# Twelve up columns of the dense expert product move into the gate-table stage; the rest runs sixteen columns ahead of the downs, whose sums stay in six PSUM banks

## The chip, the cores and the metric

One core of one Trainium2 chip runs the whole kernel in one launch. The time is device microseconds of that core. Each core has TensorE (matmuls, PE), VectorE (DVE), ScalarE (ACT), GpSimd (POOL) and SyncE (SP, which only issues transfers), an SBUF of 128 partitions, and PSUM with eight banks of 512 fp32 words per partition, into which TensorE writes.

## The reference, cut to what matters

Two layers over 512 tokens of width 1024. Each is a mixer (local attention and a long convolution, gated and projected) and then the expert block that this change is about:

```python
def block(xb):                                  # xb: tokens x 1024, after RMSNorm
    q = (xb @ w_query).reshape(c, 8, 2, 128)
    s = jnp.einsum('chpd,pkd->chpk', q, sub_keys)
    s_top, i_top = lax.top_k(s, 16)
    ...                                         # 16 of 16384 experts per head: idx, softmax weights g
    u = jnp.take(expert_u, idx, axis=0)
    act = jax.nn.gelu(jnp.einsum('chkd,cd->chk', u, xb), approximate=False)
    vsel = jnp.take(expert_v, idx, axis=0)
    return jnp.einsum('chk,chkd->cd', g * act, vsel)
```

All is fp32. A token picks 128 of 128 x 128 experts.

## The kernel before, in words

**Two ways to the same sum.** For the first 384 tokens (three blocks of 128, DT = 384) the block is computed densely: for each of 128 columns j of 128 experts, "up" is gelu(U_j x) for all 384 tokens, it is multiplied by a table G of the softmax weights (zero for experts not picked), and "down" adds the product with V_j. The last 128 tokens take the sparse way: GpSimd gathers their picked rows of U and V from HBM, four buffers of 512 KB (ROWS) going round, and VectorE takes a dot product per gathered row (`dot`, first half of the stage) or adds a weighted row to X (`add_row`, second half). There are 256 gathers per layer.

**fp32 products.** Each dense product is three fp32r matmuls: high x high, high x low, low x high. The high half is a cast (ScalarE, or VectorE for the weights), the low half a subtraction on VectorE. So an up column is 3 x 8 matmuls with 384 moving columns (L874), a down column 3 x 6 with 512 (L889).

**Stages.** The engines meet at numbered barriers (`arrive`, `all_at`). Behind barrier 4 is the table stage: for every token VectorE makes two one-hot rows (L1553, L1554), TensorE multiplies them into a 128 x 128 slice of G (L856), eight banks going round, ScalarE copies it into GST (L1095), and SP stores half tables of 64 tokens to HBM (L488). The one-hots lie in a ring of four groups of eight tokens (OHR). Two U loads and the first two V loads are issued at its start, since their buffers lie apart from those of the stage. Behind barrier 5 is the expert stage. Columns go in groups of four (JG); four up columns are ahead of the downs, in banks 0 to 3. A down takes one output block at a time, twelve matmuls over the four columns of the group, into banks 4 to 7 in turn, and VectorE adds each finished block to X (L1620), six per group.

**Order.** It is written out by hand for each engine and kept by semaphores. In the expert stage a step is a group: TensorE `step`, L894, alternates `up` (L866) and `down` (L878); ScalarE, L1128, does `split_u`, `split_v`, `gelu`; VectorE, L1622, does `split_u`, `split_v`, `weigh` (multiply with the table, cast to high, subtract to low), rows, `add_output`; SP, L497, issues U, V and the table (`load_g`, 768 KB per group); GpSimd's gathers (L573) wait until their buffer was used.

## Time and profile before

| | |
|---|---|
| runs | 3986.62 us median of 3 (3986.41 to 3987.67) |
| profiled execution | 3987.45 us, span 3985.5 us |
| busy share of the span | PE 89%, PEld 71%, DVE 73%, ACT 30%, POOL 22% |
| granted TensorE clock, mean | 0.956 |
| L874 (ups), three groups of 2048 matmuls | 405.8, 399.4, 396.5 us busy |
| L889 (downs), three groups of 1536 | 414.9, 416.5, 412.2 us busy |
| L1620 (adds of down blocks to X) x384 | 263.0 us busy |
| HBM | 672 MB read, 52 MB written, mean 182 GB/s |

Share of busy time is over both layers and all stages; a stage has its own bound. A clock of 1.0 is the full 2.4 GHz. "PEld" is the load of the stationary operand, beside the matmuls. In the timeline a row's "x8" merges eight instructions, and the brackets give the engine's idle time before it and what ended it.

### The profile page before, as it was taken

The page shows a single profiled execution, that of the slowest core. Times are in us where ns is not written, and L with a number is a line of the kernel's source. Part 1 is how long each engine was busy: PE and PEld are TensorE (multiplying, and loading weights), DVE is VectorE, ACT ScalarE, POOL GpSimd, SP SyncE. Part 2 cuts the span into 40 slices and gives each one's busy share as a digit, 9 for nine tenths or more (in the row PEclk, how much of TensorE's full clock was granted, in tenths as well). Part 3 has the DMA queues.
Part 4 walks back from the last instruction along what each step waited for, and adds up shares of the span by engine and source line. Part 5 has one row for each costly group of instructions (what it writes and reads, how often), then busy time and mean ns, then how long its engine had stood idle before and what let it go on. Part 6 is the DMA issues. An engine that isn't in the chain of part 4 may idle for free.

```text
span 3985.5 us, 50340 instructions
## 1 busy us (share of the span) xinstructions
PE 3539.7 (89%) x16330; PEld 2844.3 (71%) x16330; DVE 2925.5 (73%) x6669; ACT 1204.4 (30%) x1804; POOL 896.5 (22%) x661
## 2 busy tenths in 40 slices
PE   7899986468999999999988999845699999999997
PEld 4436753358999999999844377424589999999996
DVE  2443359997888888888724443799978888888887
ACT  2312213353333333333223032224533333333332
POOL 0000007002333333333300000160023333333332
PEclk9989998799999999999999899978999999999999
DMA  3112310236777777777521133103387777777775
GB/s 120 57 32 64 100 66 1 104 149 260 280 276 276 276 276 276 276 276 276 198 95 57 32 80 101 49 1 127 136 299 277 276 276 276 277 275 277 278 277 179
DMA packets 239738, 725.62 MB, mean 182 GB/s; under 512 B 16216, under 2 KB 116824, under 8 KB 204572
## 3 DMA queue, kind: packets, MB, share of 16 engines
q1 hardware_dynamic: 165884, 455.99, 30.4%
q0 software_dynamic: 73760, 268.47, 20.5%
q8 instruction: 48, 0.79, 0.1%
q14 instruction: 46, 0.38, 0.0%
HBM read 671.97 MB, written 52.43 MB: 182 GB/s over the span
## 4 chain that ended last, share of the span: by engine, by line
PE 77%; DVE 16%; ACT 2%; DMA 2%; issue 1%; POOL 1%; SPq 0%; DVEq 0%; POOLq 0%; ACTq 0%
PE ps L874 26%; PE ps L889 26%; PE ps L768 9%; DVE OHS L1554 5%; PE ps L637 4%; DVE OHS L1553 4%; PE ps L818 3%; PE ps L624 2%; PE ps L731 2%; PE ps L756 2%; PE ps L747 1%; PE ps L694 1%; DMA g_table<-GST 1%; PE ps L667 1%; POOL EQ L557 1%
## 5 line engine op out<-in xcount | busy, mean ns | idle before, releaser
L573 POOL DMA_INDIRECT ROWS<-u_rows_dram,GIS x256 | 352.1, 1375 | 704.0 <-DVE STG L1597 640.8
L573 POOL DMA_INDIRECT ROWS<-v_rows_dram,GIS x256 | 345.8, 1351 | 690.0 <-DVE X L1613 635.5
L1120 ACT CAST VHI<-VRAW 128x512 fp32r<-128x512 f32 x512 | 291.8, 619 | 468.9 <-PE ps L889 468.9
L889 PE MATMUL ps<-VHI,WHI 128*128 128x512 f32 x1536 | 414.9, 392 | 2.8 <-DVE WLO L1591 2.8
L889 PE MATMUL ps<-VLO,WHI 128*128 128x512 f32 x1536 | 416.5, 393 | 0.0
L874 PE MATMUL ps<-XHI,UHI 128*128 128x384 f32 x2048 | 405.8, 340 | 11.4 <-DVE ULO L1569 11.4
L889 PE MATMUL ps<-VHI,WLO 128*128 128x512 f32 x1536 | 412.2, 390 | 0.0
L1126 ACT ACTIVATE AC<-ps 128x384 f32<-128x384 f32 x256 | 126.0, 492 | 931.8 <-PE ps L874 931.7
L1620 DVE TENSOR_TENSOR X<-ps,X 128x512 f32<-128x512 f32 x384 | 263.0, 687 | 186.2 <-PE ps L889 186.2
L874 PE MATMUL ps<-XLO,UHI 128*128 128x384 f32 x2048 | 399.4, 336 | 0.0
L874 PE MATMUL ps<-XHI,ULO 128*128 128x384 f32 x2048 | 396.5, 334 | 0.0
L874 PEld LDWEIGHTS ps<-XHI,UHI 128*128 128x128 f32 x2048 | 370.4, 189 | 31.9 <-DVE ULO L1569 12.4
L874 PEld LDWEIGHTS ps<-XLO,UHI 128*128 128x128 f32 x2048 | 362.1, 189 | 0.0
L874 PEld LDWEIGHTS ps<-XHI,ULO 128*128 128x128 f32 x2048 | 359.1, 188 | 0.0
L856 PE MATMUL ps<-OHS 128*128 128x128 f32 x1536 | 232.1, 298 | 126.3 <-DVE OHS L1554 126.2
L889 PEld LDWEIGHTS ps<-VLO,WHI 128*128 128x128 f32 x1536 | 288.6, 188 | 64.8
L889 PEld LDWEIGHTS ps<-VHI,WLO 128*128 128x128 f32 x1536 | 288.9, 188 | 63.1
L1613 DVE SCALAR_TENSOR_TENSOR X<-ROWS,STG,X 128x1024 f32<-128x1024 f32 x256 | 327.0, 1277 | 3.6 <-DMA ROWS<-v_rows_dram,GIS 3.5
L1577 DVE TENSOR_TENSOR VLO<-VRAW,VHI 128x512 fp32r<-128x512 f32 x512 | 329.5, 685 | 0.0
L1569 DVE TENSOR_TENSOR ULO<-URAW,UHI 128x1024 fp32r<-128x1024 f32 x256 | 312.2, 1221 | 15.4 <-ACT UHI L1108 10.6
L1597 DVE CUSTOM_DVE_ANT_0 ROWS<-ROWS,XG 128x1024 f32<-128x1024 f32 x256 | 311.6, 1217 | 14.9 <-DMA ROWS<-u_rows_dram,GIS 14.9
L889 PEld LDWEIGHTS ps<-VHI,WHI 128*128 128x128 f32 x1536 | 284.4, 188 | 46.7 <-issue 3.4
(237 smaller groups left out, 4896.4 us busy)
## 6 DMA issues: line engine op xcount, KB each, us to landing
URAW<-ut_dram SPq DMA_DIRECT2D x128, 1024.0 KB
VRAW<-v_dram SPq DMA_DIRECT2D x128, 1024.0 KB
g_table<-GST SPq DMA_DIRECT2D x12, 4096.0 KB, 11.2
GT<-g_table SPq DMA_DIRECT2D x64, 768.0 KB, 10.0
WR<-w_in_dram SPq DMA_DIRECT2D x8, 2048.0 KB, 13.1
WR<-w_in_dram SPq DMA_DIRECT2D x32, 512.0 KB, 4.7
WR<-w_q_dram SPq DMA_DIRECT2D x8, 2048.0 KB, 8.0
WR<-w_out_dram SPq DMA_DIRECT2D x4, 2048.0 KB, 8.1
```

The lines of the kernel that those rows point to most:

```text
L573: pool.indirect_dma_start(out=ROWS[:, k % GR, :], out_offset=None, in_=table, in_offset=bass.IndirectOffsetOnAxis(ap=GIS[:, par, k:k + 1], ...
L768: last = nc.tensor.matmul(ps[:, bank, :], lhs[a], rhs[c], start=(i == 0 and k == 0), stop=(i == 2 and k == len(pairs) - 1))
L856: last = nc.tensor.matmul(ps[:, n % 8, k * NK:(k + 1) * NK], OHS[:, q % OHR, 0, 4 * s + k, :], OHS[:, q % OHR, 1, 4 * s + k, :], start=Tru ...
L874: last = nc.tensor.matmul(ps[:, jj, 0:DT], a[:, jj, k, :], c[:, k, :], start=(i == 0 and k == 0), stop=(i == 2 and k == KC - 1))
L889: last = nc.tensor.matmul(ps[:, 4 + (g0 + o) % 4, :], a[:, par, jj, b * P:(b + 1) * P], c[:, dh, jj, :], start=(n == 0), stop=(n == 3 * JG ...
L1120: nc.scalar.copy(VHI[:, dh, jj, :], VRAW[:, dh, jj, :]).then_inc(v_hi, 1)
L1554: last = nc.vector.tensor_scalar(OHS[:, q % OHR, 1, c, :], iota, IDS[:, 1, t:t + 1], IDS[:, 2, t:t + 1], ALU.is_equal, ALU.mult)
L1569: nc.vector.tensor_tensor(ULO[:, jj].rearrange("p k i -> p (k i)"), URAW[:, jj // 2, jj % 2, :], UHI[:, jj].rearrange("p k i -> p (k i)"). ...
L1577: nc.vector.tensor_tensor(VLO[:, dh, jj, :], VRAW[:, dh, jj, :], VHI[:, dh, jj, :].bitcast(F32), ALU.subtract).then_inc(v_split, 1)
L1597: nc.vector.tensor_tensor_reduce(ROWS[:, k % GR, :], ROWS[:, k % GR, :], XG[:], 1.0, 0.0, ALU.mult, ALU.add, accum_out=STG[:, par, k:k + 1 ...
L1613: nc.vector.scalar_tensor_tensor(X[:, NB - 1, :], ROWS[:, k % GR, :], STG[:, par, k:k + 1], X[:, NB - 1, :], ALU.mult, ALU.add).then_inc(r ...
L1620: nc.vector.tensor_tensor(xb, ps[:, 4 + (par * NOUT + o) % 4, :], xb, ALU.add).then_inc(out_free, 1)
```

## The change

Columns are handled in pairs (64 pairs, NP). Six pairs (EARLY), twelve columns, have their ups in the table stage: after each group of eight tokens TensorE does six of the 24 matmuls of an up column, in banks 0 and 1, and the table uses banks 4 to 7 only. The one-hot ring shrinks from four groups to two, the loops of 128 tokens are unrolled, and the copy of indices (IDS) goes. The gelu outputs are kept in a ring of sixteen columns (AC), weighed in place, with the low half in place as well (ACL on AC, ULO on URAW, VLO on VRAW). The ups run eight pairs ahead of the downs. A down takes one column at a time, three matmuls into each of six banks (2 to 7), which hold the sums over all 128 columns; X gets them once at the end. The high half of the weights is now a cast on ScalarE. Casts and differences handle a pair (128x2048, or 128x768 for weights) at once. U has four buffers of 1 MB, loaded from the time that the queries' weights are done with; V has four, at addresses used by the table stage (slots 0 and 1 under GST, 2 and 3 behind it), so its first load is issued behind barrier 5. The four rows of a pair are used in a burst at the end of VectorE's step. The last eight pairs have downs alone.

The diff, cut to its core (SP, then TensorE, ScalarE, VectorE):

```diff
-TOK_IT = 128
 CB = 64
-OH, OHR = 8, 4
+OH, OHR = 8, 2
+GB = 4
 JG = 4
 NG = NK // JG
 DB = 3
 DT = DB * P
 NOUT = 2 * DB
+UPB = 8 - NOUT
+NP = NK // 2
+AHEAD = 8
+NQ = DT // OH
+EARLY = NQ // 8
+US, VS, HS2 = 4, 4, 2
+assert UPB == 2 and EARLY == AHEAD - 2 and CB == 8 * OH and NP == 64 and AHEAD == 2 * US == 2 * VS
...
+    AC, _ = sb("AC", [P, 2 * AHEAD, DT])
+    ACL, _ = sb("ACL", [P, 2 * AHEAD, DT], F32R, offset=def_at)
+    ef_at = at[0]
+    GST, _ = sb("GST", [P, 2, NK, CB])
     OHS, _ = sb("OHS", [P, OHR, 2, OH, NK])
-    IDS, _ = sb("IDS", [P, 3, TOK_IT])
-    GST, _ = sb("GST", [P, 2, NK, CB])
+    IDXT, idxt_at = sb("IDXT", [P, 3, DT])
...
+    URAW, _ = sb("URAW", [P, US, 2, KC, P], offset=wr_at)
+    ULO, _ = sb("ULO", [P, US, 2, KC, P], F32R, offset=wr_at)
+    UHI, _ = sb("UHI", [P, HS2, 2, KC, P], F32R, offset=wr_at + 8 * US * DM)
...
+    v_at = max(at[0], ef_at + 8 * NK * CB - 16 * DM)
+    VRAW, _ = sb("VRAW", [P, VS, 2, 2, 512], offset=v_at)
+    VLO, _ = sb("VLO", [P, VS, 2, 2, 512], F32R, offset=v_at)
...
+                sp.wait_ge(pq_out, HP)
+                for p in range(US):
+                    load_u(p, p)
...
+                for h in range(DT // CB):
+                    sp.wait_ge(g_bank_free, CB // 4 * (h + 1))
+                    sp.dma_start(gd[h].rearrange("i j c -> i (j c)"),
+                                 GST[:, h % 2].rearrange("p j c -> p (j c)")).then_inc(g_stored[h % 2], 16)
+                    sp.wait_ge(u_done, 2 * h + 2)
+                    load_u(h + US, h % US)
...
+                load_v(0, 0, 2)
+                load_v(0, 1, 3)
                 g_all_stored(sp)
                 sp.nop().then_inc(sp_at_f, 1)
                 load_g(0, 0)
+                load_v(1, 0, 0)
+                load_v(1, 1, 1)
                 load_g(1, 1)
+                UN = EARLY + US
+                def step(o, g0, i):
+                    p = o + i
+                    if not isinstance(p, int) or p + UN < NP:
+                        sp.wait_ge(u_done, p * 2 + 2 * EARLY + 2)
+                        load_u(p + UN, (i + UN) % US)
+                    if i % 2 == 1 and (not isinstance(p, int) or p // 2 + 2 < NG):
+                        sp.wait_ge(wf_ready, p + 1)
+                        load_g(g0 + i // 2 + 2, i // 2 % 2)
+                    if not isinstance(p, int) or p + VS < NP:
+                        sp.wait_ge(v_out, p * 2 + 2)
+                        load_v(g0 + i // 2 + 2, i % 2, (i + 2) % VS)
...
+                def up(p, i, jj, n0=0, n1=3 * KC):
+                    j = p * 2 + jj
+                    if n0 == 0:
+                        pe.wait_ge(u_split, p + 1)
+                        if not isinstance(j, int) or j >= UPB:
+                            pe.wait_ge(act_ready, j - (UPB - 1))
+                    for n in range(n0, n1):
+                        a, c, k = PASSES[n]
+                        last = nc.tensor.matmul(ps[:, jj, 0:DT], a[:, i % (US if a is ULO else HS2), jj, k, :], c[:, k, :],
+                                                start=(n == 0), stop=(n == 3 * KC - 1))
+                    if n1 == 3 * KC:
+                        last.then_inc(u_done, 1)
+                def down(p, i, jj):
+                    if jj == 0:
+                        pe.wait_ge(w_ready, p + 1)
+                        pe.wait_ge(v_split, p + 1)
+                    wh, wl = WHI[:, (2 * i + jj) % (2 * HS2)], ACL[:, (2 * i + jj) % (2 * AHEAD)]
+                    vh, vl = VHI[:, i % HS2], VLO[:, (i + 2) % VS]
+                    for o in range(NOUT):
+                        dh, b = divmod(o, DB)
+                        for n, (a, c) in enumerate(((wh, vh), (wh, vl), (wl, vh))):
+                            last = nc.tensor.matmul(ps[:, UPB + o, :], a[:, b * P:(b + 1) * P], c[:, dh, jj, :],
+                                                    start=(isinstance(p, int) and p + jj + n == 0),
+                                                    stop=(isinstance(p, int) and 2 * p + jj == NK - 1 and n == 2))
+                    last.then_inc(v_out, 1)
+                for q in range(NQ):
+                    for s in range(OH // 4):
+                        n = q * (OH // 4) + s
+                        pe.wait_ge(oh_ready, n + 1)
+                        if n >= GB:
+                            pe.wait_ge(g_bank_free, n - (GB - 1))
+                        for k in range(4):
+                            last = nc.tensor.matmul(ps[:, 4 + n % GB, k * NK:(k + 1) * NK], OHS[:, q % OHR, 0, 4 * s + k, :],
+                                                    OHS[:, q % OHR, 1, 4 * s + k, :], start=True, stop=True)
+                        last.then_inc(g_out, 1)
+                    up(q // 8, q // 8, q // 4 % 2, q % 4 * 6, q % 4 * 6 + 6)
...
+                def step(o, i, more=True):
+                    for jj in range(2):
+                        down(o + i, i, jj)
                         if more:
+                            up(o + (i + AHEAD), i, jj)
...
+                for p in range(EARLY, AHEAD):
+                    for jj in range(2):
+                        up(p, p, jj)
+                for i in range(8):
+                    step(0, i)
+                with pe.Fori(1, NP // 8 - 1) as it:
+                    for i in range(8):
+                        step(it * 8, i)
+                for i in range(8):
+                    step(NP - 8, i, more=False)
...
+                    for n in range(q * (OH // 4), (q + 1) * (OH // 4)):
+                        h, c = divmod(4 * n, CB)
+                        act.wait_ge(g_out, n + 1)
+                        if c == 0 and h >= 2:
+                            act.wait_ge(g_stored[h % 2], 16 * (h // 2))
+                        nc.scalar.copy(GST[:, h % 2, :, c:c + 4].rearrange("p j c -> p c j"),
+                                       ps[:, 4 + n % GB, :].rearrange("p (c j) -> p c j", c=4)).then_inc(g_bank_free, 1)
+                    if q % 8 == 2:
+                        split_u(q // 8 + 1, q // 8 + 1)
+                    if q % 4 == 1 and q >= 5:
+                        j = q // 4 - 1
+                        gelu(j // 2, j // 2, j % 2)
+                gelu(EARLY - 1, EARLY - 1, 1)
...
+                def step(o, i):
+                    p = o + i
+                    if not isinstance(p, int) or p + AHEAD + 1 < NP:
+                        split_u(o + (i + AHEAD + 1), i + AHEAD + 1)
+                    if not isinstance(p, int) or p + 1 < NP:
+                        split_v(o + (i + 1), i + 1)
+                        high_w(o + (i + 1), i + 1)
+                    if not isinstance(p, int) or p + AHEAD < NP:
+                        for jj in range(2):
+                            gelu(o + (i + AHEAD), i + AHEAD, jj)
+                split_u(EARLY + 1, EARLY + 1)
+                act.wait_ge(g_stored[0], 16 * ((DT // CB + 1) // 2))
+                split_v(0, 0)
+                for jj in range(2):
+                    gelu(EARLY, EARLY, jj)
+                split_u(AHEAD, AHEAD)
+                gelu(AHEAD - 1, AHEAD - 1, 0)
+                high_w(0, 0)
+                gelu(AHEAD - 1, AHEAD - 1, 1)
...
+                    if q >= OHR:
+                        dve.wait_ge(g_out, OH // 4 * (q - OHR + 1))
+                    for c in range(OH):
+                        t = q * OH + c
+                        nc.vector.tensor_scalar(OHS[:, q % OHR, 0, c, :], iota, IDXT[:, 0, t:t + 1], None, ALU.is_equal)
+                        last = nc.vector.tensor_scalar(OHS[:, q % OHR, 1, c, :], iota, IDXT[:, 1, t:t + 1],
+                                                       IDXT[:, 2, t:t + 1], ALU.is_equal, ALU.mult)
+                        if c % 4 == 3:
+                            last.then_inc(oh_ready, 1)
+                    if q % 8 == 4:
+                        split_u(q // 8 + 1, q // 8 + 1)
...
+                def step(o, g0, i, rows):
+                    p, s, par = o + i, g0 + i // 2, i // 2 % 2
+                    if rows is add_row and i % 2 == 0:
+                        stage_weights(s, par)
+                    if not isinstance(p, int) or p + 1 < NP:
+                        n = i + 1
+                        weigh(o + n, n, (o + n) // 4 * 16 + 16 if isinstance(o, int) else o * 4 + (n // 4 * 16 + 16))
+                    if not isinstance(p, int) or p + AHEAD + 1 < NP:
+                        split_u(o + (i + AHEAD + 1), i + AHEAD + 1)
+                    if not isinstance(p, int) or p + 1 < NP:
+                        split_v(o + (i + 1), i + 1)
+                        low_w(o + (i + 1), i + 1)
+                    for k in range(4):
+                        rows(s, par, 4 * (i % 2) + k)
+                    if rows is dot and i % 2 == 1:
+                        keep_dots(s, par)
+                split_u(EARLY + 1, EARLY + 1)
+                split_v(0, 0)
+                split_u(AHEAD, AHEAD)
+                weigh(0, 0, 16)
+                low_w(0, 0)
...
+                for o in range(NOUT):
+                    dh, b = divmod(o, DB)
+                    xb = X[:, b, 512 * dh:512 * dh + 512]
+                    dve.wait_ge(v_out, NK)
+                    nc.vector.tensor_tensor(xb, ps[:, UPB + o, :], xb, ALU.add)
```

## Rows read from the trace of the kernel before

**Rows 1.** The page's chain that ended last: share of the span by engine and line

```profile
PE ps L874 26%; PE ps L889 26%; PE ps L768 9%; DVE OHS L1554 5%; PE ps L637 4%; DVE OHS L1553 4%; PE ps L818 3%; PE ps L624 2%; PE ps L731 2%; PE ps L756 2%; PE ps L747 1%; PE ps L694 1%; DMA g_table<-GST 1%; PE ps L667 1%; POOL EQ L557 1%
```

**Rows 2.** Windows of 50 us: stretch, busy us (instructions) per engine, clock, DMA share, GB/s

```profile
850.00:900.00 50.00, 33.32 (x217) 28.61 (x216) 49.87 (x220) 28.02 (x27) 0.00 (x0) 0.93 0.39 168
1200.00:1250.00 50.00, 50.00 (x255) 45.50 (x254) 42.85 (x73) 15.23 (x24) 17.32 (x13) 1.00 0.78 283
```

**Rows 3.** Timeline, half a group, expert stage, layer 1: start us, us, engine, line, operation

```profile
1934.25 1.57 PE L874 MATMUL ps<-XHI,UHI 128*128 128x384 f32 x8
...
1935.66 1.55 PE L874 MATMUL ps<-XLO,UHI 128*128 128x384 f32 x8
...
1938.44 1.08 PE L889 MATMUL ps<-VHI,WHI 128*128 128x512 f32 x4
...
1950.86 1.57 PE L874 MATMUL ps<-XHI,UHI 128*128 128x384 f32 x8
```

**Rows 4.** Four lines over the whole span: ns min/median/max, first and last start

```profile
L1569 DVE TENSOR_TENSOR ULO<-URAW,UHI x256: 1215/1220/1227, 912.1 to 3921.4; 128x1024 fp32r<-128x1024 f32 x128
...
L1577 DVE TENSOR_TENSOR VLO<-VRAW,VHI x512: 680/685/691, 934.8 to 3952.0; 128x512 fp32r<-128x512 f32 x171
...
L1613 DVE SCALAR_TENSOR_TENSOR X<-ROWS,STG,X x256: 1271/1277/1286, 1476.6 to 3963.5; 128x1024 f32<-128x1024 f32 x128
...
L1126 ACT ACTIVATE AC<-ps x256: 480/492/496, 923.5 to 3939.9; 128x384 f32<-128x384 f32 x128
```

**Rows 5.** Timeline of the table stage, layer 1

```profile
729.13 0.23 DVE L1541 CAST GI<-GIF 128x128 int32<-128x128 f32 x1
...
732.04 0.29 DVE L1553 TENSOR_SCALAR OHS<-CST,IDS 128x128 f32<-128x128 f32 x1
...
734.00 4.78 PE L856 MATMUL ps<-OHS 128*128 128x128 f32 x24 [3.44 <-DVE OHS L1554]
...
790.66 0.55 DVE L1547 COPY IDS<-IDXT 128x384 f32 x1 [0.61 <-DVE OHS L1554]
...
791.35 0.29 DVE L1553 TENSOR_SCALAR OHS<-CST,IDS 128x128 f32<-128x128 f32 x1
...
908.25 0.37 DVE L1554 TENSOR_SCALAR OHS<-CST,IDS 128x128 f32<-128x128 f32 x1
...
908.68 1.16 PE L856 MATMUL ps<-OHS 128*128 128x128 f32 x8 [0.65 <-DVE OHS L1554]
909.87 1.01 ACT L1095 COPY GST<-ps 128x512 f32<-128x512 f32 x1 [0.78 <-PE ps L856]
```

**Rows 6.** Timeline from the table stage into the expert stage, layer 1

```profile
911.06 0.33 SPq L488 DMA_DIRECT2D g_table<-GST  x1
...
913.42 2.93 PE L874 MATMUL ps<-XHI,UHI 128*128 128x384 f32 x8 [3.58 <-DVE ULO L1569]
...
918.56 1.55 PE L874 MATMUL ps<-XHI,ULO 128*128 128x384 f32 x8
...
922.56 1.07 SPq L475 DMA_DIRECT2D GT<-g_table  x2
...
923.84 7.40 SPq L468 DMA_DIRECT2D URAW<-ut_dram  x2
...
932.54 1.04 ACT L1108 CAST UHI<-URAW 128x1024 fp32r<-128x1024 f32 x1 [7.20 <-DMA URAW<-ut_dram]
```

**Rows 7.** DMA issues of the page: KB each, us from issue to landing

```profile
g_table<-GST SPq DMA_DIRECT2D x12, 4096.0 KB, 11.2
```

**Rows 8.** Timeline of the end of the expert stage, layer 1

```profile
1972.84 3.01 POOL L573 DMA_INDIRECT ROWS<-v_rows_dram,GIS  x1 [1.19 <-DVE X L1613]
...
1976.16 0.94 POOL L573 DMA_INDIRECT ROWS<-v_rows_dram,GIS  x1 [0.30 <-issue]
...
1982.89 1.07 PE L889 MATMUL ps<-VHI,WLO 128*128 128x512 f32 x4
...
1986.13 1.28 DVE L1613 SCALAR_TENSOR_TENSOR X<-ROWS,STG,X 128x1024 f32<-128x1024 f32 x1
```

318 lines of the change are left out of this document (91 added, 227 removed).

## The prediction

> **What bounds the kernel now.** I read the chain of waits first, then windows, then the timeline at three seams. The chain is TensorE's two expert lines for 52%, then the one-hots of VectorE for 9% [rows 1]. So two stretches per layer matter. In the table stage (E, 732.04 to 911 in layer 1) VectorE is busy 49.87 of 50 us and TensorE 33.32, with a granted clock of 0.93 [rows 2]: VectorE sets the pace, TensorE has a third of the time free. In the expert stage (F, 913.42 to 1987.41) TensorE is busy 50.00 of 50 us at clock 1.00, VectorE 42.85, the DMA engines 0.78 of the time [rows 2]. The reader should see that what leaves TensorE in F is worth its full price, and what is added to VectorE in E costs its full price.
>
> **TensorE's price of a column.** Ups start at 1934.25 and the next downs at 1938.44: 24 up matmuls take 4.19 us, 0.174 each. From 1934.25 to 1950.86 lie two ups and three of the six down blocks of a group, that is two columns in 16.61 us, 8.305 each [rows 3]. So the downs of a column take 8.305 - 4.19 = 4.115 us.
>
> **Stage E.** Added on VectorE: six differences of 128x2048 (pairs 1 to 6; pair 0 is before the stage). 128x1024 takes 1.22 and 128x512 0.685 [rows 4], so 0.535 for each 512 elements and 1.22 + 2 x 0.535 = 2.29 us for 2048; six are 13.7. Removed: the copies of the indices. Each of the two inside the loop costs a wait of 0.61, the copy of 0.55 and the restart until 791.35, where one-hots follow every 0.23 us: 1.4 us in all, 2.8 for two [rows 5]. The first copy goes too, but pair 0's difference comes before the stage on VectorE: GI is written at 729.36, plus 2.29 and a handshake of 0.3 is 731.95, and the first one-hot stood at 732.04 [rows 5]: nothing gained or lost. The last one-hot ends at 908.62 now [rows 5], so at 908.6 - 2.8 + 13.7 = 919.5.
>
> Does TensorE keep up? It gets 12 columns, 288 up matmuls, six after every eight tokens. Warm: 16 one-hot records in 2 x 1.16 us at most [rows 5] and 6 x 0.174 = 1.04, together 3.4; VectorE needs 3.62 for the same eight tokens (48 such groups in 176.6 - 2.8 us). So the ring of two instead of four is enough, by a narrow margin, and VectorE's splits give TensorE rest. ScalarE adds six wide casts (at most 2 x 1.04 each) and 12 gelus of 0.49 beside 96 copies of 1.01 [rows 4 to 6], some 116 us of 188: hidden, with four banks for a copy every 1.8 us. The stores and U loads in SP's order have 30 us per half table.
>
> The last one-hot matmuls then end near 920.7, the six ups at 921.7, ScalarE's copy at 921.8 and the last gelu at 922.4. TensorE can start F at once, because pair 6 is already split; today it waits for a cast and a difference, from 911.06 to 913.42 [rows 6]. F's first matmul: 922.6, that is 9.2 later.
>
> **Start of F.** Ahead of the first down stand pairs 6 and 7 (four columns). V can't be loaded early any more, since its slots lie where the table stage works. V of pair 0 is issued at about 922.6, behind the last store on SP's queue, issued at 922.0 and landing after 11.2 [rows 6, 7]: 933.2. Then 1 MB: the U load issued at 923.84 behind 1.5 MB issued at 922.56 lets ScalarE go on at 932.54, 2.5 MB in 10.0 us [rows 6]; I take 3.3 us: 936.5. ScalarE waits for it in its own order (split_v ahead of gelu of pair 6), and column 14 needs a bank that this gelu empties. So TensorE does pair 6 until 931.0, then stands still until 936.5 + 1.9 (cast) + 0.5 (gelu) = 938.9, and comes back at the low clock: today sixteen ups after the pause take from 913.42 to 918.56, 0.32 each, 2.35 more than warm [rows 6]. Pair 7: 8.4 + 2.3, so downs begin at 949.6. The weights of pair 0 are ready by then: table load issued at 933.4, landed near 943, weigh 0.95, cast 0.9, difference 0.95, 947. Bounds: if loads of one queue share rather than queue, TensorE goes on until 939.4, waits for weights until about 944 and is cold again: 946.4, 3 better; if the table load lands 10 us later than 943, the weights are ready at 957, 8 worse.
>
> **The run of F.** Per pair TensorE needs 16.61. VectorE: weigh and low_w of 128x768, 0.685 + 0.27 = 0.95 each; two splits of 2.29; four rows of 1.28 [rows 4]: 11.6 against 43/50 of 16.6 = 14.2 today, as the adds out of the banks and the cast of the weights go. ScalarE: two casts of 2, high_w 0.9, two gelus of 0.5: 6. The waits: ScalarE's split of U is released when up of the pair before the last ends, at the start of a step; it is ready on VectorE 5 us in and needed 20 us in. Low_w is ready about 8.3 us in and needed at 16.6. SP waits for the downs of each pair, about 12.4 in, and then issues V, U and at every second step the table; behind that wait stand only loads needed 20 us later or more. Rows now come four in a burst; from the last use to the next burst are 11 us for four gathers. So I price the run at TensorE's rate: 112 ups and 128 downs are 469.3 + 526.7 = 996 us, to 1945.6. The bank of the downs changes six times per column where it was 1.5 times. The only seam that rows show is from downs to ups: the first eight ups, to 1935.66, take 1.41, and the sixteen after them 2.78, or 1.39 per eight [rows 3]: 0.02. So a change of bank costs between 0 and 0.02, 4.5 x 0.02 x 128 = 12 us per layer (a gain is excluded, as the array's work is the same). I take 0, as twelve matmuls into one bank were accumulated like the three are now.
>
> **The end of F.** The last eight pairs have downs alone: 16.61 - 2 x 4.19 = 8.23 on TensorE. VectorE needs 0.95 + 2.29 + 0.95 + 4 x 1.28 = 9.3. It enters about one step ahead; followed through the eight, TensorE loses 2.4 us and VectorE finishes the rows 2.1 us and six adds, at the 0.685 of a 512-wide difference, another 4.1 us after the last matmul, 6.2 together, against 1987.41 - 1983.96 = 3.45 today [rows 8]. And the gathers: one that VectorE leaves alone is issued in 0.94 us, one behind adds and differences that read two operands from SBUF in 3.01 [rows 8]. With VectorE never idle, four cost between 4 x 0.94 and 4 x (3.01 + 0.30) = 13.2 a pair. I take 2 each with the time to land after the last one: a period of 10, 5 us more over the eight; bounds 0 and 8 x (13.2 - 9.3) = 31.
>
> The Trainium skill has another view of this row (SBUF — State Buffer, its part on the shared port pair): a VectorE tensor_tensor should not stall a gather's issue, since descriptor writing needs the write interface only, while 2-port copies do. The 3.01 beside 0.94 speaks against it here. By it the 5 us would go.
>
> **Sum, layer 1.** The last matmul: 1945.6 + 2.4 + 5 = 1953.0, the end of F 1959.2, against 1987.41: 28.2 less. In parts: ups out of F -50.3, E and its seam +9.2, tail +10.2 (2.4 + 5 + 6.2 - 3.45), and +2.7 for the start, where today some 8 us are lost and then 10.2 (949.6 - 922.6 - 16.8). Layer 2 is the same work: 56.4 less in all. The profiled execution took 3987.45 (span 3985.5, 2 us around it), so 3931.0 there; the runs shown have a median of 3986.62, 0.8 less: **3930**.
>
> **Rivals.**
> *The gathers' issue isn't held up* (the tail goes at VectorE's 9.3): 5 less per layer, 3920. For it: 0.94 stands in the same tail, with VectorE at adds out of the banks. Against: the 3.01. Chance 0.12. This is what the rule of the Trainium skill named above comes to.
> *Bank seams*: 12 per layer, 3954. For: a seam costs 0.02 now. Against: no row shows it belongs to banks. 0.10.
> *The gathers set the tail*: 26 more per layer, 3982, no measurable change. For: wide differences hold on for 2.29. Against: the 3.01 is rare. 0.05.
> *Slower: the clock stays low in E.* Cold, 24 one-hot records took 4.78 [rows 5], so sixteen take 3.2, and six ups 1.93: 5.1 us per eight tokens where VectorE, splits included, needs 3.9. Through a ring of two VectorE waits for it. All 48 groups cold: 58 per layer, 4046. It decides from about half of them: 24 x 1.2 = 29, which is the gain of a layer. For: the clock was 0.93 in a window of E. Against: TensorE will be busier in E, not less. 0.08.
> The Trainium skill (TensorE: Matmul & The Clock Gate, "A second HAM failure mode: psum-queue depth-cycling") warns of short idle spells between groups in cycling banks, which is this case; by it some of E would be cold, with the 4046 of this rival as the end. The 0.93 is all that a row shows of it.
>
> **Numbers.** Forecast 0.62 (own range 3911 to 3951), the rivals as above, unnamed 0.03. A measurement tells about 0.2%, 8 us, from no change. Faster: 0.62 + 0.12 + 0.10 + 0.01 = 0.85; within: 0.05 + 0.01 = 0.06; slower: 0.09. The range of 8 in 10 takes in the start bounds, bank seams and part of the tail: 3905 to 3966.
>
> **What would show it.** E about 11 us longer with VectorE near 50 of 50; TensorE near 45 of 50 there. A pause of TensorE of about 8 us within the first 20 us of F, released by ScalarE's activation. 16.6 us per pair after it, clock 1.00. In the last 75 us of F, gathers of over 1.5 us and TensorE waits for low_w. Wrong if E stretches by 20 or more, if a pair takes over 16.8, or if VectorE waits for rows in the run.

## The result, and the profile after

The changed kernel takes **3964.73 us** (median; 3963.13 to 3969.73), the kernel before 3986.41 (3984.25 to 3987.67): ratio 0.995, 95% interval 0.9939 to 0.9961. It is 21.7 us faster; 56.4 had been forecast. The direction held, the size did not: the time lies above the forecast's own range of 3911 to 3951, and just inside the 3905 to 3966 given for 8 in 10. The profiled execution took 3967.61 (span 3965.8), 2.9 above the median, and the working below is in its time.

The chain of the page (share of the span, by engine and line) has the shape of [rows 1], and two new links, gathers and V loads:

```profile
PE ps L869 24%; PE ps L884 24%; PE ps L778 9%; DVE OHS L1590 5%; PE ps L647 4%; DVE OHS L1589 4%; PE ps L828 3%; PE ps L634 2%; DMA ROWS<-v_rows_dram,GIS 2%; PE ps L741 2%; PE ps L766 2%; PE ps L757 1%; DMA VRAW<-v_dram 1%; DVE ULO L1574 1%; PE ps L704 1%
```

Windows of layer 1 (columns as in [rows 2]): three in the table stage E, one in the run of F, one in the tail, where downs stand alone.

```profile
750.00:800.00 50.00, 41.85 (x279) 39.39 (x280) 50.00 (x214) 30.18 (x31) 0.00 (x0) 0.93 0.37 148
800.00:850.00 50.00, 39.93 (x282) 36.99 (x280) 50.00 (x205) 30.96 (x31) 0.00 (x0) 1.00 0.43 169
850.00:900.00 50.00, 41.86 (x289) 39.28 (x287) 50.00 (x213) 31.22 (x31) 0.00 (x0) 0.97 0.50 197
1200.00:1250.00 50.00, 50.00 (x252) 45.12 (x251) 32.96 (x38) 16.00 (x15) 15.64 (x15) 1.00 0.80 282
1900.00:1950.00 50.00, 43.18 (x170) 33.55 (x169) 40.22 (x34) 12.71 (x10) 29.51 (x21) 0.93 0.88 309
```

In E, VectorE is at 50.00 and TensorE went from 33.32 to between 39.9 and 41.9, with the clock at 0.93 to 1.00. In the run VectorE fell from 42.85 to 32.96. The last row is the surprise: TensorE at 43.18 of 50, with the DMA engines 0.88 busy.

**The start of F**, timeline of layer 1 (start us, us, engine, line, operation, idle before and what ended it), to be held against [rows 6]:

```profile
918.93 0.35 SPq L493 DMA_DIRECT2D g_table<-GST  x1
919.46 0.33 SPq L476 DMA_DIRECT2D URAW<-ut_dram  x1
919.48 1.66 PE L869 MATMUL ps<-XHI,UHI 128*128 128x384 f32 x8 [0.61 <-ACTq L368]
...
919.89 2.33 SPq L481 DMA_DIRECT2D VRAW<-v_dram  x2
...
932.12 0.38 SPq L485 DMA_DIRECT2D GT<-g_table  x1
...
937.72 1.90 ACT L1106 CAST VHI<-VRAW 128x2048 fp32r<-128x2048 f32 x1 [15.94 <-DMA VRAW<-v_dram]
...
940.15 2.90 PE L869 MATMUL ps<-XHI,UHI 128*128 128x384 f32 x8 [12.07 <-ACT AC L1117]
...
944.43 0.95 DVE L1615 TENSOR_TENSOR AC<-AC,GT 128x768 f32<-128x768 f32 x1
...
950.13 0.39 PE L884 MATMUL ps<-VHI,WHI 128*128 128x512 f32 x1
```

SP issues the store of the table, then a U load, then V. ScalarE waits 15.94 us for V, the gelus stand behind that cast, and TensorE stops for 12.07 us. From F's first matmul to the first down pass 30.65 us.

**The run**, timeline of TensorE, against [rows 3]:

```profile
1201.53 0.39 PE L884 MATMUL ps<-VHI,WHI 128*128 128x512 f32 x1
...
1205.72 1.57 PE L869 MATMUL ps<-XHI,UHI 128*128 128x384 f32 x8
...
1209.91 0.39 PE L884 MATMUL ps<-VHI,WHI 128*128 128x512 f32 x1
...
1218.29 0.39 PE L884 MATMUL ps<-VHI,WHI 128*128 128x512 f32 x1
```

Ups still take 4.19 (1205.72 to 1209.91), but the 18 downs of a column 4.19 too (1201.53 to 1205.72) and not 4.115: about 0.233 each. A pair takes 16.76 for 16.61, without any wait.

**The tail.** First the timeline of TensorE, VectorE and POOL from the end of the last ups to the final adds, against [rows 8]; then a window of it (columns as in [rows 2]); then what the engines waited for in that stretch (us in total, times, longest); then its DMA issues (count, KB, median us to landing).

```profile
1888.68 0.39 PE L884 MATMUL ps<-VHI,WHI 128*128 128x512 f32 x1
...
1905.71 1.29 DVE L1644 SCALAR_TENSOR_TENSOR X<-ROWS,STG,X 128x1024 f32<-128x1024 f32 x1 [2.05 <-DMA ROWS<-v_rows_dram,GIS]
...
1912.90 2.28 DVE L1604 TENSOR_TENSOR VLO<-VRAW,VHI 128x2048 fp32r<-128x2048 f32 x1
...
1913.17 2.84 POOL L583 DMA_INDIRECT ROWS<-v_rows_dram,GIS  x1 [0.30 <-issue]
...
1915.10 0.95 DVE L1622 TENSOR_TENSOR ACL<-AC,WHI 128x768 fp32r<-128x768 f32 x1
...
1916.11 0.64 PE L884 MATMUL ps<-VHI,WHI 128*128 128x512 f32 x1 [2.06 <-DVE ACL L1622]
...
1972.46 3.67 DVE L1688 TENSOR_TENSOR X<-ps,X 128x512 f32<-128x512 f32 x6
```

```profile
1910.00:1920.00 10.00, 7.94 (x28) 5.99 (x27) 9.34 (x9) 2.73 (x2) 7.03 (x5) 0.83 1.02 371
```

```profile
DVE X L1644 <- DMA ROWS<-v_rows_dram,GIS: 12.0, 9, 4.2
...
PE ps L884 <- DVE ACL L1622: 7.7, 5, 3.2
```

```profile
VRAW<-v_dram SPq DMA_DIRECT2D x4, 1024.0 KB, 8.0
GT<-g_table SPq DMA_DIRECT2D x2, 768.0 KB, 14.3
ROWS<-v_rows_dram,GIS POOLq DMA_INDIRECT x28, 6.1
```

VectorE waits for rows nine times, and TensorE behind it five times for the low half of the weights. From 1888.68 to the end of the adds (1972.46 + 3.67 = 1976.13) pass 87.4 us, where TensorE alone needs 16 x 4.19 = 67. Of the rest 7.7 are its waits and, as the starts of its matmuls show, 3.3 the low clock behind the two longest of them (0.83 on average in the window above; eight downs there come 0.43 apart); 8.5 lie between the end of its last matmul (1967.64) and the end of the adds.

**Where the forecast went, layer 1.** F was to end at 1959.2 and ends at 1976.13, 16.9 later: the stage before E gave 2.5 and E 0.6, the start of F cost 3.6 more (30.65 for 27.0), the run 56 x 0.15 = 8.4, the tail 8.0 (87.4 for 1959.2 - 1953.0 + 8 x 8.23 + 2.4 + 5 = 79.4). In layer 2 F takes 1056.0, as in layer 1 (1056.65). Forecast were 1036.6.

### The profile page after: what moved, and what is told of

Same layout as the page of the kernel before. It is cut to its first block, busy times and chain, and to the rows that moved or that the text cites. A ratio compares the mean times of both kernels' runs of the same rounds, so it can differ in the third digit from the quotient of the medians.

```text
span 3965.8 us, 45690 instructions
## 1 busy us (share of the span) xinstructions
PE 3541.4 (89%) x16330; PEld 2840.3 (72%) x16330; DVE 2528.3 (64%) x5267; ACT 1235.1 (31%) x1420; POOL 813.7 (21%) x661
## 4 chain that ended last, share of the span: by engine, by line
PE 74%; DVE 17%; DMA 3%; ACT 3%; issue 2%; POOL 1%; DVEq 0%; SPq 0%; POOLq 0%; ACTq 0%
PE ps L869 24%; PE ps L884 24%; PE ps L778 9%; DVE OHS L1590 5%; PE ps L647 4%; DVE OHS L1589 4%; PE ps L828 3%; PE ps L634 2%; DMA ROWS<-v_rows_dram,GIS 2%; PE ps L741 2%; PE ps L766 2%; PE ps L757 1%; DMA VRAW<-v_dram 1%; DVE ULO L1574 1%; PE ps L704 1%
## 5 line engine op out<-in xcount | busy, mean ns | idle before, releaser
L1574 DVE TENSOR_TENSOR ULO<-URAW,UHI 128x2048 fp32r<-128x2048 f32 x128 | 293.4, 2292 | 603.7 <-ACT UHI L1098 603.6
L884 PE MATMUL ps<-VHI,WHI 128*128 128x512 f32 x1536 | 611.5, 398 | 14.8 <-DVE ACL L1622 14.8
L884 PE MATMUL ps<-VLO,WHI 128*128 128x512 f32 x1536 | 609.2, 397 | 0.0
L884 PE MATMUL ps<-VHI,ACL 128*128 128x512 f32 x1536 | 605.2, 394 | 0.0
L583 POOL DMA_INDIRECT ROWS<-u_rows_dram,GIS x256 | 323.4, 1263 | 742.7 <-DVE STG L1628 653.8
L583 POOL DMA_INDIRECT ROWS<-v_rows_dram,GIS x256 | 301.1, 1176 | 683.1 <-DVE X L1644 596.9
L884 PEld LDWEIGHTS ps<-VHI,ACL 128*128 128x128 f32 x1536 | 289.7, 189 | 71.9
L1604 DVE TENSOR_TENSOR VLO<-VRAW,VHI 128x2048 fp32r<-128x2048 f32 x128 | 292.5, 2285 | 55.9 <-ACT VHI L1106 55.9
L1590 DVE TENSOR_SCALAR OHS<-CST,IDXT 128x128 f32<-128x128 f32 x768 | 268.3, 349 | 0.0
L896 PEld LDWEIGHTS ps<-OHS 128*128 128x128 f32 x1536 | 201.8, 201 | 87.8 <-DVE OHS L1590 80.4
## 6 DMA issues: line engine op xcount, KB each, us to landing
GT<-g_table SPq DMA_DIRECT2D x64, 768.0 KB, 13.8
```

Of the source, the lines that this page charges most:

```text
L583: pool.indirect_dma_start(out=ROWS[:, k % GR, :], out_offset=None, in_=table, in_offset=bass.IndirectOffsetOnAxis(ap=GIS[:, par, k:k + 1], ...
L884: last = nc.tensor.matmul(ps[:, UPB + o, :], a[:, b * P:(b + 1) * P], c[:, dh, jj, :], start=(isinstance(p, int) and p + jj + n == 0), sto ...
L896: last = nc.tensor.matmul(ps[:, 4 + n % GB, k * NK:(k + 1) * NK], OHS[:, q % OHR, 0, 4 * s + k, :], OHS[:, q % OHR, 1, 4 * s + k, :], star ...
L1574: nc.vector.tensor_tensor(ULO[:, i % US].rearrange("p a k n -> p (a k n)"), URAW[:, i % US].rearrange("p a k n -> p (a k n)"), UHI[:, i % ...
L1590: last = nc.vector.tensor_scalar(OHS[:, q % OHR, 1, c, :], iota, IDXT[:, 1, t:t + 1], IDXT[:, 2, t:t + 1], ALU.is_equal, ALU.mult)
L1604: nc.vector.tensor_tensor(VLO[:, (i + 2) % VS].rearrange("p d j n -> p (d j n)"), VRAW[:, (i + 2) % VS].rearrange("p d j n -> p (d j n)"), ...
```

## Experiments

Times are medians, with the ratio to the kernel before, measured alongside. "After" is the changed kernel.

### The down matmuls (16.76 us a pair)

**s_six**: the downs of a pair together, six into a bank before it changes, then both ups.

```
-                    for jj in range(2):
-                        down(o + i, i, jj)
-                        if more: up(o + (i + AHEAD), i, jj)
+                    down(o + i, i)      # for o: for jj in range(2): three matmuls
+                    for jj in range(2):
+                        if more: up(o + (i + AHEAD), i, jj)
```

> The downs of a pair are done together, six matmuls into a bank before it changes (6 changes per pair instead of 12), then both ups. A pair of the run takes 16.76 us in the changed kernel (1201.53 to 1218.29) and took 16.61 before, with 3 changes. Theory 'change of bank costs': 0.15 / 9 = 0.017 us per change, so 16.66 per pair, 6.4 us less per layer, 13 less in all. Rival 'the same stationary operand twice in a row costs': still 12 such repeats per pair, 16.76, no change. Rival 'the operands' places': no change.

3964.9 (0.9947, 0.9927 to 0.9967); a down still at 0.233, a pair 16.74, where the price of bank changes would have made it 16.66.

**s_each**: the two loops of down exchanged, so the bank changes after each matmul.

```
-                    for o in range(NOUT):
-                        dh, b = divmod(o, DB)
-                        for n, (a, c) in enumerate(((wh, vh), (wh, vl), (wl, vh))):
+                    for n, (a, c) in enumerate(((wh, vh), (wh, vl), (wl, vh))):
+                        for o in range(NOUT):
+                            dh, b = divmod(o, DB)
```

> The same 18 matmuls of a down column in the order of the operand pairs, the bank changes after every one (36 changes per pair instead of 12). Theory 'change of bank costs' 0.017 each: 16.76 + 24 x 0.017 = 17.16 us per pair, 26 us more per layer, 51 more in all. Rival 'same stationary operand twice in a row': no repeats are left, so 16.61 per pair and 19 us less in all. Rival 'the operands' places': no change.

3959.03 (0.9932, 0.9912 to 0.9952). In TensorE's timeline six downs of one kind take 1.38 to 1.40; a pair is 16.69. That is less than in after, but not the 16.61 of the rival.

```profile
1204.27 1.56 PE L884 MATMUL ps<-VLO,WHI 128*128 128x512 f32 x6
1205.67 1.54 PE L884 MATMUL ps<-VHI,ACL 128*128 128x512 f32 x6
1207.05 1.57 PE L869 MATMUL ps<-XHI,UHI 128*128 128x384 f32 x8
```

Three times as many bank changes, and faster: the price of a bank change is ruled out in both directions.

**s_apart**: order (wh, vh), (wl, vh), (wh, vl), so no stationary operand comes twice running.

> Within a bank the order is high x high, low x high, high x low, so the same weights are never loaded twice in a row; bank changes stay at 12 per pair. Theory 'change of bank costs': 16.76, no change. Rival 'same stationary operand twice in a row': 16.61 per pair, 9.6 us less per layer, 19 less in all.

3956.73 (0.9926, 0.9907 to 0.9946); a pair 16.71, again not 16.61. A stationary operand used twice running isn't what makes a down dear: s_apart saves its 0.05 a pair in the first four downs behind the ups, and then goes at after's rate. It shows best in the last eight pairs, where no ups stand between. Timeline of TensorE, two downs of s_apart that lie 36 apart, then two of s_each 18 apart, then two of before 24 apart:

```profile
1888.81 0.39 PE L884 MATMUL ps<-VHI,WHI 128*128 128x512 f32 x1
...
1897.21 0.39 PE L884 MATMUL ps<-VHI,WHI 128*128 128x512 f32 x1
```

```profile
1891.47 1.52 PE L884 MATMUL ps<-VHI,WHI 128*128 128x512 f32 x6
...
1895.60 1.52 PE L884 MATMUL ps<-VHI,WHI 128*128 128x512 f32 x6
```

```profile
1967.48 1.07 PE L889 MATMUL ps<-VHI,WHI 128*128 128x512 f32 x4
...
1972.92 1.07 PE L889 MATMUL ps<-VHI,WHI 128*128 128x512 f32 x4
```

That is 0.2333 a down in s_apart, as in after (1888.68 to 1897.08 for 36), 0.2294 in s_each and 0.2267 in before. Where each down reads another pair of tiles than the one before it, it comes at 0.2333; in sixes and fours on the same two tiles it comes sooner.

**s_start**: each bank is restarted in each column; the output then lacks the sum over columns.

```
-  start=(isinstance(p, int) and p + jj + n == 0), stop=(... and n == 2))
+  start=(n == 0), stop=(n == 2))
```

> Each down bank is restarted with every column (its first matmul of three overwrites, the third closes the group), so nothing is summed over columns; the output differs. Theory (adding to a sum in a bank costs more than writing it anew, and after never writes anew): the down matmul falls from 0.2333 to 0.230 or less, a pair from 16.76 to 16.6. Rival (the summing costs nothing, as before also summed eleven of twelve): 0.2333, 16.76 a pair, 3960 to 3968.

3962.45 in one run; a pair 16.76 (downs from 1202.93 and from 1219.69). Summing without a restart costs nothing.

**s_one**: the loops of s_each, and all of a pair into the bank `UPB + i % NOUT`; the six outputs are mixed.

> All 36 down matmuls of a pair go to one bank, and all matmuls of one kind (high with high, low with high, high with low) come behind each other, so that six follow in one kind and one bank, as near to before's four as this kernel allows; the six outputs are summed into each other, so the output differs. Theory (kind order and bank together make before's 0.2265 to 0.230): the down matmul comes at 0.228 on average, a pair at 16.58 to 16.63. Rival (neither has to do with it): 1.39 for six as with a change of bank after each, 16.70 a pair.

3957.79 in one run; TensorE's timeline:

```profile
1208.75 1.55 PE L884 MATMUL ps<-VHI,WHI 128*128 128x512 f32 x6
...
1212.91 1.57 PE L869 MATMUL ps<-XHI,UHI 128*128 128x384 f32 x8
```

The next column's downs start at 1217.10, a pair is 16.69, like s_each: the one bank adds nothing. So the order of the operands gives 0.07 of the 0.15 a pair; why it does, and why before's order is better by another 0.08, stays open. The times of s_each, s_apart and s_one alone (two runs, two and one) hardly tell them from after; it is the pair in the trace that does.

### The start of F

**a_gelu_first**: ScalarE's gelus of pair 6 ahead of its cast of V.

```
-                split_v(0, 0)
                 for jj in range(2):
                     gelu(EARLY, EARLY, jj)
+                split_v(0, 0)
```

> ScalarE does both gelus of pair 6 ahead of the cast of V's first pair. TensorE's pause of 12.07 us in front of pair 7 (released by that gelu) goes. Theory 'the table's way through HBM is late next': the table store was issued at 918.93 and landed 13.1 later, its load is issued at 932.12, weights are ready near 947, so TensorE pauses in front of the first down instead, near 936 to 948, and runs cold afterwards: first down at 949 to 950 instead of 950.13, total less by 0 to 3 us. Rival 'the order of ScalarE is what costs': first down 12 us earlier, 24 us less in all.

3960.66 (0.9939, 0.9922 to 0.9955). The pause goes from the ups of pair 7 to the first down; timeline of TensorE:

```profile
947.79 0.79 PE L884 MATMUL ps<-VHI,WHI 128*128 128x512 f32 x1 [10.76 <-DVE ACL L1622]
```

It shrinks by 1.3 only. Behind the wait for V lay a second one, for the table's way through memory: V landed at 938.6, the table at 943.5, and the weights of pair 0 need both.

**a_start**: the queue of SP and both engines in the order in which things land.

```
 SP:      store, V(0), table, +U(9), +V(1)     (was: store, U(9), V(0), V(1), table)
 ScalarE: +gelus of pair 6, +split_u(8), +gelu(7, 0), split_v(0)   (was: split_v(0) first)
 VectorE: +split_u(8), split_v(0)              (was: split_v(0), split_u(8))
```

> The start of the expert stage in another order. SP: V of pair 0, then the table load as soon as the table is stored, and only then U of pair 9 and V of pair 1. ScalarE: gelus and the cast of pair 8 ahead of V's cast; VectorE: pair 8's difference ahead of V's. Theory 'transfers of one queue wait for those issued before': store 11.5, table load some 6 us after it, weights ready near 941, first down 21 to 24 us after the first up instead of 30.65, 7 to 10 less per layer, 14 to 20 in all. Rival 'the store itself is slow whatever stands beside it, and the rest is compute': 3 less per layer, 6 in all.

3954.67 (0.9923, 0.9907 to 0.994). Its timeline: first matmul, ScalarE's cast of V, first down.

```profile
919.13 1.68 PE L871 MATMUL ps<-XHI,UHI 128*128 128x384 f32 x8 [0.62 <-ACTq L368]
...
935.41 1.90 ACT L1108 CAST VHI<-VRAW 128x2048 fp32r<-128x2048 f32 x1 [2.98 <-DMA VRAW<-v_dram]
...
942.41 0.79 PE L886 MATMUL ps<-VHI,WHI 128*128 128x512 f32 x1 [6.35 <-DVE ACL L1624]
```

From first matmul to first down 23.3 us for 30.65, in layer 2 22.7. Part of it is given back: TensorE stops for 6.35 us, and the downs behind come at the low clock (0.43 apart), so that F as a whole is 6.4 and 6.2 us shorter. The 14 to 20 us expected in all were 10.1. What remains is V, which lands at 935.4, behind the store; the table lands at 937.5, and VectorE's difference of V lasts until 939.6, where the weighing starts.

**n_no_early**: the twelve early columns go back into F; all else stays.

```
-                    up(q // 8, q // 8, q // 4 % 2, q % 4 * 6, q % 4 * 6 + 6)
...
-                for p in range(EARLY, AHEAD):
+                for p in range(AHEAD):
```

> The twelve early columns go back: no up, split or gelu in the table stage, sixteen ups ahead of the first down in the expert stage. All else stays as changed. Theory: the table stage is 13.7 us shorter (six differences of 2.29), the expert stage has 12 x 4.19 = 50.3 us of ups more, but 67 us of ups now cover the way of the table through HBM, so the pause of 12.07 us and its cold matmuls (30.65 us from the first up to the first down where the ups alone take 16.8) go: -13.7 + 50.3 - 13.9 = 22.7 more per layer, 45 more than the changed kernel's 3964.7, 4010. Rival (the prediction's own sum, in which the start cost 10.2): 26 per layer, 53 more. Rival 'the start's pause does not depend on the early columns': 36.6 per layer, 73 more.

4019.6 (1.0084, 1.0067 to 1.0101): 55 slower than after, and slower than before. The price of the prediction's own sum (53) fits, that of the theory (45) doesn't. In layer 1, E is 13.8 us shorter (176.2 for 190.0), the way to the first down 41.3 longer (71.9 for 30.65). TensorE's work on twelve columns is 50.3; the way to the first down grows by 9 less, since the longer ring in F covers the landing of V and of the table. That is what moving them ahead gave away. The rest of the change, taken without them, costs 33 us.

### The tail

**t_no_rows**: the last 32 rows of a layer are neither gathered nor added; the output lacks them.

```
-                for o in (NP - 16, NP - 8):
-                    for i in range(8):
-                        step(o, o // 2, i, add_row)
+                for i in range(8):
+                    step(NP - 16, NP // 2 - 8, i, add_row)
+                for i in range(8):
+                    step(NP - 8, NP // 2 - 4, i, None)
```

> Leaves out 32 of the 128 gathered V rows per layer and their adds: the last eight pairs have downs, weights and V splits alone. The end of the stage takes 87.4 us in layer 1 now (1888.69 to 1976.13). Theory 'the rows make the end slow': 8 x 8.38 + 4.1 = 71, 16 less per layer, 33 in all. Rival 'the down matmuls and handshakes between ScalarE and VectorE make it slow': little change, 0 to 8 in all.

3935.42 (0.9874, 0.9854 to 0.9894), 29.3 less than after; in the window of the tail TensorE does not stop, and the tail takes 71.1 us.

```profile
1900.00:1950.00 50.00, 50.00 (x216) 40.25 (x215) 23.31 (x17) 13.99 (x12) 0.00 (x0) 1.00 0.36 114
```

So the rows are the whole loss of the tail, by VectorE's time for them and by the waits for them together. The next four kernels move them.

**t_rows664**: six rows a pair at pairs 32 to 47, four at 48 to 55, none in the last eight.

```
+                        step(it * 8, it * 6 + (GSTEPS - 24), i, add_row, 6)
+                for o, per in ((NP - 16, 4), (NP - 8, 0)):
```

> The 128 V rows per layer are spread otherwise: six per pair in pairs 32 to 47, four in 48 to 55, none in the last eight, where it was four throughout. Nothing is left out. Theory 'VectorE and the DMA engines have the room in the run': VectorE 11.6 + 2.56 = 14.2 of 16.76 us, traffic (4.4 + 1.0) MB in 16.76 us = 322 GB/s where 369 were seen in the end: pairs stay at 16.76 and the end shrinks by 16 per layer, 33 in all. Rival 'bursts of six rows come late': pairs 32 to 47 take 1 us more each, 16 per layer, and nothing is left of the gain.

3973.4 (0.9968, 0.9957 to 0.998): missed, and 8.7 slower than after. The tail is clean, and the loss stands where the rows went. VectorE's waits from 1500 to 1850:

```profile
DVE X L1644 <- DMA ROWS<-v_rows_dram,GIS: 72.5, 40, 7.0
```

**t_spread**: four rows a pair as in after, two behind the weighing and two at the end of the step.

```
                         weigh(o + n, n, ...)
+                    for k in range(2):
+                        rows(s, par, 4 * (i % 2) + k)
...
-                    for k in range(4):
+                    for k in range(2, 4):
```

> As after, but VectorE takes its four rows of a pair in two halves: two right behind the weighing, two behind the low half of the weights. Nothing else moves. Theory (in the last sixteen pairs VectorE waits for the fourth row of a burst, because four buffers are refilled only as the burst goes on): the waits for rows in the tail, 12.0 us in layer 1 of after, shrink to under 5, and each layer is 4 to 8 us shorter: 3949 to 3957. Rival (in the tail the transfers themselves are the limit, 7.4 MB in 20 us at 1900 to 1920, and no order of the rows helps): 3962 to 3968, as after.

3962.27 (0.9937, 0.992 to 0.9953), the rival's figure. In the last pairs the waits for rows are 14.1 us, where after has 12.0: it wasn't the burst that made them.

**t_spread664**: both edits together, in halves of three.

> Six rows at each of pairs 32 to 47, four at 48 to 55, none at the last eight, as in the kernel that took them in bursts of six, and now in two halves of three, behind the weighing and behind the low half. Theory (that kernel lost its 29 us again because rows five and six of a burst waited a round trip of a gather, 6 to 7 us, for buffers): VectorE waits under 1 us per half, TensorE stays at 49.9 of 50 between 1550 and 1800, the last matmul comes 14 to 16 us per layer earlier than in after: 3932 to 3942. Rival (the transfers are the limit, 0.88 to 0.90 busy at 308 to 318 GB/s in that stretch, because six rows of 0.5 MB beside U and V are more than come in a pair): the waits stay above 20 us per layer, 3960 to 3975.

3959.35 (0.9929, 0.9912 to 0.9945): close to the rival again. VectorE's waits from 1500 to 1735, the gathers of that stretch, and two windows:

```profile
DVE X L1644 <- DMA ROWS<-v_rows_dram,GIS: 51.8, 34, 5.2
```

```profile
ROWS<-v_rows_dram,GIS POOLq DMA_INDIRECT x79, 7.2
```

```profile
1500.00:1735.00 235.00, 226.64 (x1126) 202.82 (x1125) 181.35 (x142) 74.13 (x68) 117.06 (x89) 1.00 0.89 321
```

```profile
1900.00:1950.00 50.00, 50.00 (x220) 40.80 (x220) 23.37 (x18) 16.20 (x13) 0.00 (x0) 1.00 0.45 137
```

**t_spread5**: five rows at pairs 32 to 55, one in the last eight, in halves.

```
+                for n, per in enumerate((5, 5, 5, 1)):
+                    for i in range(8):
+                        step(NP // 2 + 8 * n, GSTEPS + 5 * n, i, add_row, per)
```

> As after, with five rows a pair at pairs 32 to 55 and one a pair in the last eight, in halves of two and three. Theory (six rows a pair are more than the transfers bring: 0.9 busy at 302 to 327 GB/s and 49 us of waits for rows between 1550 and 1850; four leave 0.75 to 0.80 at 266 to 281 GB/s): five need half a megabyte more in 16.7 us than four, some 300 GB/s, 0.84 busy; VectorE's waits for rows stay under 10 us there, TensorE at 50 of 50, and the tail keeps its gain: 3938 to 3946. Rival (it is the four buffers and a landing of 6 us, which hold at five rows as well): waits of 20 us and more between 1550 and 1850, 3950 to 3960.

3935.62 (0.9879, 0.9864 to 0.9894), the same as with the rows left out. The same stretch, 1500 to 1735, VectorE's waits and the window:

```profile
DVE X L1644 <- DMA ROWS<-v_rows_dram,GIS: 59.3, 14, 6.3
```

```profile
1500.00:1735.00 235.00, 235.00 (x1180) 212.23 (x1179) 172.69 (x135) 74.44 (x70) 107.37 (x78) 1.00 0.86 305
```

The time came out 2.4 us under the range, the reason given for it only in part. VectorE waits longer than at six rows, 4.2 us in each of 14 pairs (under 10 us in all had been expected), and TensorE doesn't stop at all. The waits stand ahead of the low half of the weights, in the first half of the rows (timeline, VectorE and then TensorE's next pair):

```profile
1609.51 1.28 DVE L1644 SCALAR_TENSOR_TENSOR X<-ROWS,STG,X 128x1024 f32<-128x1024 f32 x1 [4.23 <-DMA ROWS<-v_rows_dram,GIS]
...
1615.12 0.95 DVE L1622 TENSOR_TENSOR ACL<-AC,WHI 128x768 fp32r<-128x768 f32 x1
...
1620.11 0.39 PE L884 MATMUL ps<-VHI,WHI 128*128 128x512 f32 x1
```

What decides is how far VectorE is ahead. With four rows a pair the low half is ready 8.9 us before TensorE's downs of that pair, in after and in all of these kernels before pair 32. With five this lead falls to about 4 (1616.07 to 1620.11 here) and stays over 1.0 in both layers. With six it falls to 0.1 again and again from the fourth pair on, in halves (t_spread664) as in one burst behind the low half (t_rows664), and TensorE waits. There 235 us bring 79 gathers where 14 pairs want 84, 0.94 of it; TensorE is at 226.64 of 235, 0.96. Whether the lack is the DMA engines' rate (321 GB/s, 0.89 busy) or four buffers with 7.2 us to land these runs don't tell apart.

### Together

**c_spread**, **c_spread664** and **c_spread5** take a_start, s_each and one of the three placings of the rows.

> The start order of the kernel that loads the weights' table ahead of U(9) and V(1) (3954.7), the down matmuls with a change of bank after each (3959.0), and rows in halves of two. If the three add: 3967 less 12 (start) less 6 (matmuls) less 8 to 16 (halves of rows): 3933 to 3942. If the rows' halves give nothing: 3947 to 3951. If the matmul order gave nothing real either: 3952 to 3956.

> The same start and matmul order with 6, 4 and 0 rows a pair, in halves. If the burst was what cost: 3967 less 12 less 6 less 29: 3918 to 3926. If the transfers are the limit: 3948 to 3960, no better than the kernel with the start order alone.

> The start order, the down matmuls with a change of bank after each, and 5, 5, 5 and 1 rows a pair in halves: the last one's result less 17 to 20, as measured for these two edits with four and with six rows: 3920 to 3928. If five rows a pair wait like six: 3934 to 3940.

3941.81 (0.9888, 0.9871 to 0.9904), 3936.0 (0.9875, 0.9859 to 0.9892) and **3911.39** (0.9816, 0.9803 to 0.983). The first is at the top of its range; the second is better than the transfers' case and worse than the bursts'; the third is 24.2 under t_spread5, 53 under after and under its range too. In layer 1 its adds end at 1950.17, for 1976.13.

## Why the prediction was right or wrong, step by step

**What bounds the kernel: right.** What leaves TensorE in F is worth its price, what VectorE gains in E costs its price. n_no_early shows the second, 13.8 us of E for the splits of six pairs, where six times 2.29 = 13.7 had been worked out, and the first less 9: twelve columns of 50.3 make the way to the first down 41.3 longer.

**Stage E: right.** From the first one-hot (729.50) to F's first matmul 190.0 us in both layers; 190.6 had been forecast. The rival of a cold clock fell: 0.93, 1.00 and 0.97, with VectorE at 50.00. The warning of the Trainium skill (TensorE: Matmul & The Clock Gate, "A second HAM failure mode: psum-queue depth-cycling") did not come true here: TensorE was busy 40 to 42 of 50 us in E instead of 33.32, and the clock of these windows is 0.93 to 1.00, where it was 0.93 [rows 2].

**Start of F: the mechanism right, the size not.** The step was "V of pair 0 is issued at about 922.6, behind the last store", from which followed 936.5 for its landing. V was issued on time for F's earlier start (919.89), but landed at 937.6, 17.8 later and not 13.9. Of these 3.9, 1.6 are the store: it landed 13.1 us after its issue, not 11.2. The rest is V's own, 5.6 us behind the store where 3.3 had been taken. Ahead of it stood the U load of pair 9, released by the last early column and issued at 919.46 between the two. It is in the diff and in the description of SP's order, and I counted it under E. Where this load doesn't stand there, V comes 3.9 (n_no_early) and 3.7 us (a_start) behind the store, so it is worth 1.7 to 1.9. The pause was 12.07 for about 8, the start 3.6 us longer a layer. a_gelu_first shows what lies behind, a_start what the whole order is worth: 10.1 us for both layers.

**The run: the step that failed first is "I take 0".** The bound of 12 us a layer was the right warning for the wrong reason. The banks cost nothing (s_each, s_six), nor does the lack of restarts (s_start). The reason given, "as twelve matmuls into one bank were accumulated like the three are now", looked at the sums and not at the operands: before ran four downs on the same two tiles, the change runs one. By the order alone a down comes at 0.2333 (after, s_apart), 0.2294 (s_each) or 0.2267 (before) where no ups stand between; why is not explained. In size it is 8.4 us a layer. That VectorE, ScalarE and SP hide in the run was right: the window stands at 50.00.

**The tail: what failed is the low clock, taken at nothing, and "6.2 together" for the finish; "5 us more over the eight" came out by luck.** TensorE's waits had been forecast at 2.4 + 5 = 7.4 us and are 7.7. Three of the five are 0.8 each, VectorE's 9.3 us a pair against 8.4: the 2.4, as worked out. The other two, 2.06 and 3.18, have the size of the 5, but another cause in the main: ahead of them VectorE waits 3.2 and 4.2 us for rows. For the time to land my period of 10 had 2 us beside four issues of 2; a gather lands after 6.1, and after 6.7 to 11.0 where it is issued between 1896 and 1930, with the DMA engines busy throughout (1.02 at 371 GB/s in the window above). The issue that I priced was there: 2.84 at 1913.17, beside VectorE's 2.28 us difference and the low half behind it, and it is this gather that lands last, 11.0 us later, its two forerunners after 7.1 and 6.7. So the hold-up can be some 2 of the 4.2. The rule of the Trainium skill (SBUF — State Buffer, its part on the shared port pair), by which such an issue would not be held, is marked there as inferred, and is not borne out by that row, as it was not by [rows 8]. The same part does let a VectorE instruction with two SBUF inputs hold up a GpSimd instruction that reads SBUF, as the gather reads its indices (GIS); no run here tells which it is.

Beyond the forecast stand 8.0 us a layer. The low clock behind the two waits is 3.3 of it: I had put such a term at the start of F and none here. The finish is 2.3: 8.5 for 6.2, as VectorE waits 2.9 us for three of the last four rows. The price of the downs, as in the run, is 1.3, the waits 0.3, and 0.8 are not assigned. t_no_rows gives 29.3 for all that the rows cost in both layers. My rival of the tail (26 more a layer) had the right place, and was too dear. Whether more buffers or fewer bytes would help in the tail isn't shown; smaller bursts don't (t_spread).

**Sum.** 2 x (3.6 + 8.4 + 8.0) = 40, less 2 x 0.6 in E, less some 2 us in the stages between: 36.7, the miss of the spans (3985.5 - 56.4 = 3929.1 for 3965.8). Each of the three stretches had been named with its bounds, and for the seams and the tail the favourable end was taken, or one near it. The middles of the bounds (2.5 more at the start, 6 for the seams, 10.5 more in the tail) add 38 for both layers and give 3968. That would have been luck: the bounds of the run were for bank changes, which cost nothing, those of the tail for issues alone. None of the three signs named for being wrong came up either.

## What to carry to other kernels

When work is thinned out at the end of a stage, look at each stream that keeps its rate per step: here four rows a pair, harmless at 16.8 us a pair, set the end at 8.4. Moving such a stream forward pays only as far as the stretch that takes it has room: five a pair cost nothing, six cost about what they saved. Read the room as a lead, from the engine's last result for a step to its first use: 8.9 us at four rows, about 4 at five, 0.1 at six. Where a wait of TensorE is forecast, ask what its clock does behind it. For a queue at a seam write down every issue in its order, the ones of the stage that ends included.

## What the runs showed of the hardware

A down matmul of 512 columns with one and the same form comes at 0.2267 to 0.2333 us at clock 1.00, by its order: 0.2333 where each reads another pair of tiles than the one before (after, s_six, s_apart, s_start), 0.2294 in sixes on the same two tiles (s_each; in s_one too, with a single bank), 0.2267 in before's fours. Neither bank changes nor restarts move it, and a stationary operand used twice running doesn't either. Over the 2304 downs of a layer the whole difference, 0.0066, is 15 us, an estimate from these three rates. Why the order matters no run here shows.

In 235 us VectorE waited 59.3 us for gathers without costing TensorE any (t_spread5), and 51.8 us cost it 8.4 (t_spread664): a sum of waits says nothing until one sees what lead it eats.

In the tail of after TensorE's clock was at its low level behind the waits of 2.06 and 3.18 us (0.83 on average from 1910 to 1920 and from 1930 to 1940), and at 1.00 behind the three of 0.8 (1940 to 1960).
